# Gathers by head and eight tokens, summed through 128x8 blocks in four column positions, in the last stage of a two-block kernel on one core

## What is computed

```python
s1 = einsum('thc,hnc->thn', q[:, :, 0], keys1)       # 128 keys a side
s2 = einsum('thc,hnc->thn', q[:, :, 1], keys2)
v1, i1 = top_k(s1, 16); v2, i2 = top_k(s2, 16)
top_s, top_pos = top_k((v1[..., :, None] + v2[..., None, :]).reshape(t, 8, 256), 16)
idx = take_along_axis(i1 * 128 + i2, top_pos)        # 16 picks for a token and head
gate = softmax(top_s)
act = gelu(einsum('thkd,td->thk', expert_u[idx], h))
out = einsum('thk,thkd->td', gate * act, expert_v[idx])
```

## Time and profile before

| | us |
|---|---|
| median of the runs (3148.14 to 3149.35) | 3149.2 |
| span of the profiled execution, first to last instruction | 3147.3 |
| first gather issued | 1760.96 |
| last gather's product starts | 3133.30 |
| PE, DVE, ACT, POOL busy over the span | 2714.7, 1357.1, 590.2, 708.3 |

### The profile page before, as it was taken

How to read it: one execution, slowest core, us unless ns; L and a number is a source line. 1 busy time by engine, 2 the same in 40 slices (tenths; PEclk the granted TensorE clock), 3 DMA queues, 4 the chain that set the end, 5 groups by cost and what they waited for, 6 DMA issues and landing times. The chain is left out here.

```text
span 3147.3 us, 27781 instructions
## 1 busy us (share of the span) xinstructions
PE 2714.7 (86%) x10052; PEld 1434.7 (46%) x10052; DVE 1357.1 (43%) x3261; ACT 590.2 (19%) x1357; POOL 708.3 (23%) x622
## 2 busy tenths in 40 slices
PE   8999697877888888769989899999988888888887
PEld 5755343333333333244768666666543343333332
DVE  2162300000000000044531676667777777777774
ACT  2132100000000000022120222322322322222222
POOL 0000000000000000001420233334434444444442
PEclk9899799999888999979999999999999999999989
DMA  4002699999999999531224799999999999999997
GB/s 146 27 21 113 263 426 426 427 426 426 426 424 423 420 418 421 251 137 47 94 67 149 290 426 425 425 418 421 400 426 427 412 426 426 427 414 426 420 421 329
DMA packets 138856, 1049.63 MB, mean 334 GB/s; under 512 B 22032, under 2 KB 23008, under 8 KB 48224
## 3 DMA queue, kind: packets, MB, share of 16 engines
q0 software_dynamic: 82944, 545.32, 41.5%
q1 hardware_dynamic: 55776, 502.53, 38.8%
HBM read 1051.96 MB, written 20.97 MB: 341 GB/s over the span
## 5 line engine op out<-in xcount | busy, mean ns | idle before, releaser
L2184 PE MATMUL psum<-peer_ring,peer_diag 128*128 128x512 f32 x2048 | 956.8, 619 | 154.2 <-ACT peer_diag L2245 154.1
L2037 POOL DMA_INDIRECT peer_ring<-in_peer_uv,peer_pick x512 | 576.5, 1126 | 910.7 <-PE psum L2184 746.6
L2353 DVE CUSTOM_DVE_ANT_0 peer_ring<-peer_ring,sb_rows 128x1024 f32<-128x1024 f32 x512 | 625.1, 1225 | 348.6 <-DMA peer_ring<-in_peer_uv,peer_pick 337.2
L2184 PEld LDWEIGHTS psum<-peer_ring,peer_diag 128*128 128x128 f32 x2048 | 396.6, 198 | 666.3 <-issue 430.7
L1120 PE MATMUL psum<-ffn1w_w,sb_y 128*64 128x512 f32 x1872 | 510.4, 649 | 85.9 <-DMA ffn1w_w<-in_w_up 60.0
L1165 DVE TENSOR_TENSOR sb_y<-psum,sb_y 128x512 f32<-128x512 f32 x32 | 22.1, 692 | 877.0 <-ACT sb_y L1148 877.0
L1120 PEld LDWEIGHTS psum<-ffn1w_w,sb_y 128*64 128x64 f32 x1872 | 176.1, 149 | 346.7 <-issue 345.0
L2245 ACT ACTIVATE peer_diag<-sb_ident,peer_mix 128x128 f32<-128x128 f32 x512 | 178.1, 395 | 683.7 <-DVE peer_mix L2363 681.9
L1141 PE MATMUL psum<-ffn1w_w,moe_hT 128*64 128x512 f32 x864 | 227.8, 598 | 36.0 <-DVE moe_hT L1170 33.7
L1213 POOL DMA_INDIRECT expert_rows<-sb_tiles,ffn_block_tok x32 | 32.3, 1009 | 894.6 <-ACT sb_tiles L1154 894.6
L1516 PE MATMUL psum<-sb_y,sb_tiles 128*128 128x256 f32 (+1 forms) x640 | 189.5, 455 | 17.3 <-ACT mix_Q L1741 8.9
(11 more groups left out here) (429 smaller groups left out, 2498.0 us busy)
## 6 DMA issues: line engine op xcount, KB each, us to landing
ffn1w_w<-in_w_gate SPq DMA_DIRECT2D x64, 2048.0 KB, 31.6
ffn1w_w<-in_w_down SPq DMA_DIRECT2D x54, 2048.0 KB, 35.8
ffn1w_w<-in_w_up SPq DMA_DIRECT2D x53, 2048.0 KB, 34.3
sb_tiles<-in_w_in2b SPq DMA_DIRECT2D x56, 512.0 KB
sb_rows<-in_w_up SPq DMA_DIRECT2D x11, 2048.0 KB, 36.0
sb_rows<-in_w_down SPq DMA_DIRECT2D x10, 2048.0 KB, 32.2
sb_tiles<-in_w_query SPq DMA_DIRECT2D x30, 512.0 KB
sb_tiles<-in_w_out SPq DMA_DIRECT2D x24, 512.0 KB
```

The lines of the kernel that those rows point to most:

```text
L2037: pool.indirect_dma_start(out=ring[:, slot], out_offset=None, in_=A["peer_uv"], in_offset=bass.IndirectOffsetOnAxis(ap=pick[:, i, j:j + 1] ...
L2184: last = nc.tensor.matmul(ps[:, BANK[i] + c], diag[:, b % DIAGS, x], ring[:, slot, D + 512 * c:D + 512 * (c + 1)], start=False, stop=end, ...
L2353: dve.tensor_tensor_reduce(ring[:, n % RING, 0:D], ring[:, n % RING, 0:D], hr[:, i], 1.0, 0.0, ALU.mult, ALU.add, dots[:, i, j + x:j + x + ...
```

## The change

A gather brings all 16 picks of one head for 8 tokens. Partition 16a + k of a slot holds pick k of the a-th of 8 tokens. A batch is now four gathers of one head and one `quarter`: gather r of the batch holds tokens 32r + 8 quarter to 32r + 8 quarter + 7. There are 128 batches, and still 512 gathers of 1 MiB. `RING` goes from 10 to 8, and `spent` is raised once a batch, behind its eight products.

- The batches of a tile are ordered by sets of heads, `SETS = ((1, 1, 2, 4), (8,), (4, 4), (8,))`: for each set, four quarters, and in each quarter the heads of the set.
- The dots need each token's row on 16 partitions. TensorE multiplies a 32x128 0/1 matrix (`copies`) with 32 token rows, `spread`, and ScalarE copies the result to `hb`, `spread_out`, 128x1024 a time. A pair (two gathers' rows) takes two such rounds, through the two PSUM banks that the running sums don't use. `hb` holds three pairs. 32 quads (tile, quarter, set) give 64 pairs. Three are made ahead; the others stand in `SPREADS_AT`.
- Diagonals are gone. `mixing` writes a 128x8 block for each gather, inside 24 zeros on either side; a 32-column window of it is the stationary operand, and the result goes to PSUM partitions 32r to 32r + 31, so that a batch uses four column positions.
- The picks and gates of a group must be turned from token-major to pick-major: a VectorE product with `octet` (256 elements a partition), a product and a transpose on TensorE (`turn`), the picks copied by VectorE (`picks_turned`, which raises `picked`), the gates by ScalarE (`gates_turned`).
- Scores now share PSUM bank 4 with the queries, and the queries of the first half come earlier. Late jobs stand at every second `step` (a step is two gathers); gates are made, passed through the sigmoid and merged one by one.
- The searches have an explicit plan (`SEARCH`) of steps for the three pieces.
- Four small tables instead of one are awaited before VectorE's first search (`loaded`, 80 instead of 32).

```diff
-RING = 10
+RING = 8
+BATCH, QUARTERS = 4, 4
+SETS = ((1, 1, 2, 4), (8,), (4, 4), (8,))
+SEARCH = {2: (0, 1, 2), 3: (5, 6, 8), 4: (10, 12, 13), 5: (15, 17, 18), 6: (20, 22, 23), 7: (25, 27, 28)}
+for _g in range(8, 16):
+    _s = 30 + 4 * (_g - 8)
+    SEARCH[_g] = (_s, _s + 1, _s + 3)
+for _g in range(16, 24):
+    _s = 102 + 4 * (_g - 16)
+    SEARCH[_g] = (_s, _s + 1, _s + 3)
+for _g in range(24, 32):
+    _s = 144 + 5 * (_g - 24)
+    SEARCH[_g] = (_s, _s + 2, _s + 4)
+    for r, at in zip(range(3, 8), ((0, 1, 3), (5, 6, 8), (10, 11, 13), (15, 16, 18), (20, 21, 23))):
+        for b, job in zip(at, (("query", 2 * r), ("query", 2 * r + 1), ("scores", r))):
+            JOBS_AT.setdefault(b, []).append(job)
+    for j, job in enumerate(late):
+        JOBS_AT.setdefault(2 + 2 * j, []).append(job)
...
                     if n >= RING:
-                        pool.wait_ge(spent, n - RING + 1)
+                        pool.wait_ge(spent, (n - RING) // BATCH + 1)
...
+                def spread(pair):
+                    for c in range(2):
+                        if pair or c:
+                            pe.wait_ge(hb_out, 2 * pair + c)
+                        for x in range(2):
+                            r = slice(SPAN * (2 * side + x), SPAN * (2 * side + x + 1))
+                            last = nc.tensor.matmul(ps[:, bank + x], copies[r, P * quarter:P * (quarter + 1)],
+                                                    hr[r, i, 512 * c:512 * (c + 1)], start=True, stop=True)
+                        last.then_inc(hb_ps, 1)
...
+                def weighted_sum(b):
+                    i, _, quarter = BATCH_OF[b]
+                    pe.wait_ge(mixed, b + 1)
+                    for c in range(2):
+                        for r in range(BATCH):
+                            slot = (BATCH * b + r) % RING
+                            last = nc.tensor.matmul(ps[SPAN * r:SPAN * (r + 1), sums_bank(i) + c],
+                                                    mix[:, b % DIAGS, r, EDGE - 8 * quarter:EDGE - 8 * quarter + SPAN],
+                                                    ring[:, slot, D + 512 * c:D + 512 * (c + 1)],
+                                                    start=False, stop=b == LAST_BATCH[H * i + H - 1], skip_group_check=True)
+                    last.then_inc(spent, 1)
...
                 scores(0)
                 pe.wait_ge(scaled, 1)
-                rows(0, 0)
-                rows(1, 2)
+                rows(0, 2)
+                pe.wait_ge(s_out, 1)
                 query(2)
                 query(3)
-                pe.wait_ge(r_out, 4)
+                pe.wait_ge(r_out, 2)
+                for pair in range(3):
+                    spread(pair)
                 residual(0)
-                residual(1)
                 scores(1)
+                turn(0)
...
+                def spread_out(pair):
+                    bank = spread_bank(pair)
+                    for c in range(2):
+                        act.wait_ge(hb_ps, 2 * pair + c + 1)
+                        if c == 0 and pair >= HB // 2:
+                            act.wait_ge(dotted, last_reader(pair - HB // 2) + 1)
+                        act.activation(hb[:, hb_of(pair):hb_of(pair) + 2, 512 * c:512 * (c + 1)], ps[:, bank:bank + 2],
+                                       ACT.Copy).then_inc(hb_out, 1)
...
-                rows_out(0, 0)
-                rows_out(1, 2)
+                rows_out(0, 2)
+                for pair in range(2):
+                    spread_out(pair)
                 exponentials(0)
...
-                    dve.tensor_copy(pick[:, i, h * K:(h + 1) * K], which[:]).then_inc(picked, 1)
                     dve.wait_ge(e_out, g + 1)
...
+                    step(dve.tensor_tensor(placed[:].rearrange("p s (a c) -> p s a c", c=K),
...
+                def picks_turned(g):
+                    dve.wait_ge(turned, g + 1)
+                    dve.tensor_copy(pick[:, g], ps[:, 5, P:P + K]).then_inc(picked, 1)
...
+                def product(n):
+                    dve.wait_ge(hb_out, 2 * pair + 2)
+                    dve.wait_ge(landed[n % RING], 16 * (n // RING + 1))
...
-                for b in range(BATCHES):
-                    products(b)
+                for n in range(BATCH * BATCHES):
+                    at, b = n // 2, n // BATCH
+                    product(n)
+                    if n % BATCH == 0 and b >= 1:
+                        mixing(b - 1)
```

More of the change, by code:

```diff
@@ L1904, with _batches @@
 QUERIES = 2 * PEER_H
-GA, GB, BR, OUT = (KD * n for n in range(4))
 LATE = 4 * KD
+BATCH, QUARTERS = 4, 4
+SETS = ((1, 1, 2, 4), (8,), (4, 4), (8,))
+BATCHES, PER = NT * P * PEER_H * TOPK // P // BATCH, TOPK // BATCH
+STEPS = 2 * BATCHES
+HB, GM = 6, 12
+BATCH_OF, QUADS = [], []
+def _batches():
+    for i, sizes in enumerate(SETS):
+        head = 0
+        for size in sizes:
+            for quarter in range(QUARTERS):
+                QUADS.append((i, quarter, size, len(BATCH_OF)))
+                BATCH_OF.extend((i, hd, quarter) for hd in range(head, head + size))
+            head += size
@@ new lines, with last_reader @@
+_batches()
+GROUPS = NT * PEER_H
+FIRST_BATCH = [next(b for b, (i, hd, _) in enumerate(BATCH_OF) if PEER_H * i + hd == g) for g in range(GROUPS)]
+LAST_BATCH = [max(b for b, (i, hd, _) in enumerate(BATCH_OF) if PEER_H * i + hd == g) for g in range(GROUPS)]
+QUAD_OF = [max(n for n, quad in enumerate(QUADS) if quad[3] <= b) for b in range(BATCHES)]
+def last_reader(pair):
+    quad, side = divmod(pair, 2)
+    return BATCH * (QUADS[quad][3] + QUADS[quad][2] - 1) + 2 * side + 1
+SPREADS_AT = {}
+for _quad in range(2, len(QUADS)):
+    _start, _wide = QUADS[_quad][3], QUADS[_quad - 1][2] > 1
+    SPREADS_AT.setdefault(_start - (2 if _wide else 1), []).append(2 * _quad)
+    SPREADS_AT.setdefault(_start - 1, []).append(2 * _quad + 1)
@@ L1919, in _jobs @@
     for h in range(PEER_H):
[L1920 to L1923 removed]
+        at = 98 + 4 * h
+        for b, job in ((at, ("query", QUERIES + 2 * h)), (at + 1, ("query", QUERIES + 2 * h + 1)), (at + 3, ("scores", PEER_H + h))):
+            JOBS_AT.setdefault(b, []).append(job)
@@ L1954, in peer @@
         keys = st.sb("keys", [P, 2 * H, NKEYS])
-        q = st.sb("q", [P, 2, HT])
-        near = st.sb("near", [P, H, 2, 2 * NKEYS])
-        gb = st.sb("gb", [P, KD, HT])
-        io = st.sb("iota", [P, K])
+        near = st.sb("near", [P, 3, 2, P])
+        far = st.sb("far", [P, H, 2, P])
+        work = st.sb("work", [P, 3, HT])
+        io, octet, eights = st.sb("iota", [P, K]), st.sb("octet", [P, P]), st.sb("eights", [P, K])
+        copies = st.sb("copies", [P, 4 * P])
         sc2 = st.sb("sc2", [P, 2, NKEYS])
@@ L2094, in conv_product, with turn @@
+                def turn(g):
+                    pe.wait_ge(placed_in, g + 1)
+                    if g == 0:
+                        pe.wait_ge(loaded, 80)
+                    else:
+                        pe.wait_ge(gates_out, g)
+                    nc.tensor.matmul(ps[:, 5, P:P + K], placed[:, 0], eights[:], start=True, stop=True)
+                    nc.tensor.transpose(ps[:, 5, 0:P], placed[:, 1], ident[:]).then_inc(turned, 1)
                 def conv_product(x):
@@ L2157, in _ @@
                 scores(2)
-                for b in range(BATCHES):
-                    i, j = place(b)
-                    for name, m in JOBS_AT.get(b, ()):
+                turn(1)
+                for step in range(STEPS):
+                    b = step // 2
+                    if step % 2 == 0:
+                        for pair in SPREADS_AT.get(b, ()):
+                            spread(pair)
+                    for name, m in JOBS_AT.get(step, ()):
                         if name == "query":
@@ L2291, in _ @@
                             act.activation(rs, mean, ACT.Sqrt).then_inc(late_root, 1)
-                    if at == PER // 2 and g + 2 < GROUPS:
-                        exponentials(g + 2)
-                    if g in (15, 16, 31) and at == 2:
-                        squares({15: 0, 16: 1, 31: 2}[g])
-                diagonals(BATCHES - 1)
+                    if step - 2 in PICKS_AT:
+                        gates_turned(PICKS_AT[step - 2])
+                    if step % 2 == 0:
+                        for pair in SPREADS_AT.get(b, ()):
+                            spread_out(pair)
+                    if step - 1 in EXPERTS_AT:
+                        exponentials(EXPERTS_AT[step - 1])
+                    if step % 2 == 0 and b >= 1 and BATCH_OF[b][0] != BATCH_OF[b - 1][0]:
+                        squares(BATCH_OF[b - 1][0])
+                    if step % 2 == 1:
+                        gelu(b)
                 squares(NT - 1)
@@ L2424, in _ @@
                     picks_found(g)
[L2425 to L2435 removed]
+                    if g == 0:
+                        picks_turned(0)
```

399 lines of the change are left out of this document (215 added, 184 removed).

## The result

The changed kernel takes **3491.8 us** (median of four runs, 3488.2 to 3498.1) against 3149.3 of the kernel before (four runs, 3148.1 to 3149.9). The ratio is 1.109, with a 95% interval of 1.107 to 1.110. The direction was forecast. The size was not: +343 us instead of +116, outside the range of 3178 to 3365. The profiled execution has a span of 3496.2 us.

A forecast was written before the change was run, and what follows sets the result against it. The prediction took the DMA engines at 426 GB/s as the bound, with 21 us of slack. Added costs of 139, less 21 and less 2 at the end, gave +116: 3265 us, range 3178 to 3365.

The forecast's parts named there:

- The ring: Slots freed four at a time: some 60 batches without a search cost 0.4 us more each, +24 us, bounds 0 and 90.
- First eight batches: TensorE work queued in order takes 17.0 us a batch against 12.0 of DMA: +40 us, bounds 15 and 80.
- Start: First gather waits for a chain through three engines, issued at 1777.8 instead of 1760.96: +17 us.
- Batches 8 to 15: One pair of token rows each, 10.8 us against 11.5 of DMA; +5 us given for collisions.
- Searches: More frequent searches on VectorE exceed the DMA time in three stretches of steps: +38 us, bounds 10 and 90.
- Three changes of tile: `finish` on VectorE waits for the last sum, squares and a table load: 5 us each, +15, bounds 0 and 30.
- Column positions: The weighted sum's 16 records in four column positions overlap almost wholly and take 2.2 us.
- The rival of 3417: Column positions do not overlap, so each weighted sum takes 6.9 us: 3417 us, chance 0.08.
- The diagonals and the tail: Removing ScalarE's 178 us of diagonals and TensorE's diagonal products gains nothing beside full DMA, except 2 us at the end.
- The gathers' addresses: Rival: one token's picks lie at multiples of 1 MiB or side by side, slowing gathers: +70, 3335 us, chance 0.06.
- the rival that I took it from, 3183: Only start and first batches cost, while searches, ring and tiles hide: 3183 us, chance 0.18.
- my signs of being wrong: DMA rate staying at 426 GB/s through the searches, or a batch's weighted sum far from 2 to 4 us.

The follow-up runs named there:

- edit 2: Changed kernel with only the first pair of token rows spread, later spreading products and copies left out, eight slots kept; 3432.1 us (1.090).
- edit 11: Changed kernel with `turn(0)` before the three spreads on TensorE and `exponentials(0)` before the two `spread_out` copies on ScalarE; 3503.7 us (1.112).
- edit 10: Changed kernel with the searches' VectorE instructions left out from group 8 on, so old picks are used again; 3447.9 us (1.095).
- edit 1: Changed kernel with a batch's `mixing` moved from behind the next batch's first product to behind its own last product; 3366.5 us (1.069).
- edit 9: Changed kernel whose weighted sum computes only one of its two halves of 512 columns; 3400.7 us (1.080).
- edit 8: Changed kernel with four unused 128x512 products on TensorE behind each weighted sum from batch 66 on; 3515.8 us (1.117).

## Why the prediction was wrong in size

**The ring, +24: the step that failed.** I wrote "the next gather's landing and product 2.46 + 1.31 (`mixing` is behind it)" and laid the loop over two batches: 18.9 to 20.6 us for two, 9.5 to 10.3 each. The 2.46 assumes that a next gather is in flight when the last of a batch lands. But eight slots in fours are two batches, and batch b + 2 is issued only after the sum of b, which waited for b + 1's first product: two batches are issued ahead of it, and what is left of them lands in the meantime. So each batch runs the whole turn by itself: 4.2 + 6.6 + 1.15 = 12.0. The pieces were right: from issue to product I had 1.1 + 2.0 + 2.46 = 5.6, and the loop above shows 5.87. The count was wrong, one batch in a turn and not two. With one, my own pieces give 1.31 + 0.3 + 3.6 + 5.6 = 10.8 at the slow clock, 1.0 over the DMA. The other 1.2 up to 12.0 is mostly in the mean time from issue to product, 6.6 instead of 5.6; the hand-over has 0.3 more than my pieces, the product 0.15 less. The runs price the term at 248 us (eight slots in fours instead of ten, the rest as in edit 2), where I had 24 and an upper bound of 90. What the freeing in fours costs at ten slots is not in the 248. The bound was no better than the term, since it came from a longer sum in the same wrong loop. What I should have asked is: at the moment GpSimd waits, which gathers are still in flight? In after, by the DMA packets, half a gather's bytes on the mean when a batch's first gather is issued, and under a tenth at 38 of 126 times.

**First eight batches, 17.0 us forecast, 19.5 measured.** TensorE's order was right. The timeline has four rounds, two jobs and a sum in a batch (durations and what came before, as in the loop):

```profile
1830.45 0.94 POOL L2110 DMA_INDIRECT peer_ring<-in_peer_uv,peer_pick  x1 [14.69 <-PE psum L2255]
...
1837.86 2.08 PE L2185 MATMUL psum<-sb_rows,peer_copies 32*128 32x512 f32 x4 [1.11 <-ACT peer_hb L2361]
...
1839.87 6.20 PE L2207 MATMUL psum<-sb_y,sb_tiles 128*128 128x256 f32 x16
...
1845.91 3.62 PE L2129 MATMUL psum<-sb_y,sb_tiles 128*128 128x256 f32 x16
...
1849.46 1.93 PE L2255 MATMUL psum<-peer_ring,peer_mix 128*32 128x512 f32 x16
...
1852.19 1.87 POOL L2110 DMA_INDIRECT peer_ring<-in_peer_uv,peer_pick  x1 [17.08 <-PE psum L2255]
```

The rounds take 9.8 us for four (1830.08 to 1839.87) instead of 8.3: the third and the fourth have 2.08 us instead of 1.13, and the job behind them 6.20 instead of 3.6. TensorE had idled between rounds, and its mean granted clock is 1.00 from 1830 to 1834.6 and 0.55 from there to 1845.9. I priced the clock in the last 350 us and forgot it here, where I had put the idle time in myself. The other error is the reference: I counted against 12.0 us of DMA, while before took 10.85 a batch here. The stretch cost 69 us instead of 40. Edit 2 gives back 51 of it.

**Start, +17: 21.5 on the first product, 18.8 without the later entry.** The first gather came at 1781.98, forecast 1777.8. Of these 4.2 us, 3.6 were there before the first round, which began at 1761.07 and not at 1757.5: 2.7 from the entry, and the rest mostly because the two queries took 9.1 where I had 8.3. The rounds added 1.4, again with the clock: they took 2.3 us at first and then 3.2, where I had 2.4 throughout:

```profile
1761.07 1.13 PE L2185 MATMUL psum<-sb_rows,peer_copies 32*128 32x512 f32 x4
...
1774.62 2.08 PE L2185 MATMUL psum<-sb_rows,peer_copies 32*128 32x512 f32 x4 [1.11 <-ACT peer_hb L2361]
...
1781.98 1.06 POOL L2110 DMA_INDIRECT peer_ring<-in_peer_uv,peer_pick  x1 [33.48 <-DVE peer_pick L2492]
```

The size was right. But as a term of a sum it does not stand by itself: edit 11 started the gathers 13 us earlier and nothing was gained.

**Batches 8 to 15, +5: 15.** Too low, and again through the ring: between the same two gathers the ten slots gain 10 on the eight.

**Searches, +38: 44** by edit 10. The size is right, and in part by luck. My reason was that VectorE would be near 95% busy in the three search stretches and set their pace; it is 77, 70 and 69% busy there (2046 to 2261, 2503 to 2734, 2795 to 3054). And the 44 hold with eight slots only: with ten, the searches share in the 25 us of the next term.

**Three changes of tile, +15.** No run isolates them. With ten slots and without the copies, what is left is 36 us over the kernel before, of which 11 is there at the first product (4.8 of it by the later entry) and some 25 lie behind it, searches among them. It stays open how much the tiles have of that.

**Column positions, 2.2 us forecast: 1.93.** They overlap in full; the sum of 16 records began its groups of four 0.43 us apart at full clock, and took 3.64 us at half clock, as I had put it (3.6). (The 2.5 us that I worked out from 2.38 do not follow: 6.9 / 2.38 is 2.9.) The rival of 3417 had a number near the result and is still refuted: its 6.9 us are nowhere in the trace. **The diagonals and the tail** went as said: no gain shows for the 178 us of ScalarE, and behind the last product's start the end gave back 0.9 us (349.8 of lag there, 348.9 in the spans), where I had 2.

**The gathers' addresses.** Refuted by 426 GB/s with ten slots. The Trainium skill, page "DMA: Bandwidth & Descriptors", section "Latency and other measured facts", warns of row pitches of large powers of two; no run here shows a loss of that kind.

The parts thus add up otherwise than I had them: ring 248 (3432 to 3184), copies 60 (3492 to 3432), all else 36 (3184 to 3148), together 344. These are costs in that order of removal; edit 1 shows that 125 us can also be had without a slot more. Without the ring my terms came to 92 and the runs' to 96. That is partly luck, since the first batches cost more than I had and the first gather's start is no cost by itself. The range could not hold the result either: its upper end added the bounds of the first batches and the searches and left the ring at 24. (Its lower end, 3178, is 5 under the rival that I took it from, 3183.) And my signs of being wrong did not look at the ring: the rate fell and the sum took 1.9 to 3.6 us, as forecast. The distance between the first issues of two batches, 12.0 us instead of 10.3, would have shown it.

## What to carry to other kernels

Before a ring is made shallower or freed in larger groups, write down one turn of it, from the freeing to the first use of what is then fetched, and count how many groups are in flight while the freeing waits; with two groups a turn serves one group, and its whole latency stands against one group's transfer time. What frees a slot belongs in front of the wait for the next transfer on its engine, even if it costs nothing in the deep ring. And where an added step makes TensorE wait, price the slower clock in that place too.

## What the runs showed of the hardware

This is the time from a gather's issue to its landing in after, for the 64 of the 512 gathers whose landing the trace records:

```profile
DMA to landing us min/median/max: 5.6/8.2/14.9
```

Over all 512, no product starts less than 5.48 us after its gather's issue (gather 296, 2811.30 to 2816.78). Gather 100, issued when all earlier ones had landed, took 5.6 us too. At 426 GB/s the bytes of 1.05 MB are 2.46 us of that. The Trainium skill, page "DMA: Bandwidth & Descriptors", section "Anatomy of one DMA — SWDGE (gpsimd) path", gives 2.0 us plus the bytes' time for one such transfer, an estimate of 4.4 us here; with the 0.94 us of the issuing instruction the trace agrees to within 0.3 us.

Four column positions of 32 overlap wholly: 16 records of 128x512 took 1.93 us at full clock, where 8 of 128 columns took 3.6, an estimated 3.7 times as many records in the same time.

The mean granted clock of TensorE in the late stretches, in which it idles between sums, lay between its two levels of 1.2 and 2.4 GHz: 0.59 to 0.61 in after, 0.50 in edit 9, 0.79 in edit 8. From batch 66 on the sum took 3.64 us instead of 1.93, the lower level, in after and in most batches of edit 8 alike. The fillers raised the mean and mostly not the clock of the instructions that mattered.
